# Banded attention with scores made keys by queries, shifted by maxima of rough products

## The chip, the cores and the metric

One core of a Trainium2 chip runs the whole program. The metric is the device time in microseconds (us) from start to end, the median of three runs.

## What is computed

Two layers of a hybrid block (latent attention, banded attention with a sink, a short convolution, a mixture of 16 experts), then a third block with linear and differential attention. The change touches banded attention alone. 1024 latent tokens stand beside 256 context tokens; six query heads share two key heads of 64 channels. A latent query sees all 256 context keys and the latent keys at most 128 positions away; its softmax has one more term, the head's sink. In the first layer the 256 context queries attend to the context keys too. Cut to this:

```python
valid = (jnp.abs(q_pos[:, None] - k_pos[None, :]) <= SWA_WINDOW) & ((k_pos >= 0) & (k_pos < s_len))[None, :]
s_loc = jnp.einsum('bqgrd,bkgd->bgrqk', q_b, k_b).astype(jnp.float32) * SWA_SCALE
s_loc = jnp.where(valid, s_loc, -jnp.inf)
s_ctx = jnp.einsum('bqgrd,bcgd->bgrqc', q_b, k_ctx).astype(jnp.float32) * SWA_SCALE
p = sink_softmax(jnp.concatenate([s_ctx, s_loc], axis=-1), sink).astype(v.dtype)
return (jnp.einsum('bgrqc,bcgd->bqgrd', p[..., :n_ctx], v_ctx)
        + jnp.einsum('bgrqk,bkgd->bqgrd', p[..., n_ctx:], v_b))
```

## The kernel before

The program is a row of stages, each a block in which TensorE, VectorE, ScalarE, GpSimd (POOL) and the DMA queue have their own instruction lists, tied by semaphores; a stage begins when the one before has ended on all engines. `first_half` (L1820) calls, for each of two layers, the input projection, banded attention (`window_attention`, L922), then latent attention (`latent_projections`, L1133; `latent_attention`, L1229). With `with_ctx` (first layer only) the context queries are computed as well.

Banded attention has its operands in on-chip memory: `PR` holds the projected queries and keys, channels on partitions; `SV` the values, tokens on partitions, with 64 columns of ones beside the 64 channels, so that one product gives the output and the softmax's denominator. There are no transfers in the stage. Scores must be better than one fp32r product gives, so each operand is split in a rounded part (fp32r) and the remainder. `keys` has the rounded keys twice over, on both halves of the partitions, `qs` the rounded queries in one half and their remainder in the other; their product over 128 rows (L981) is rounded keys by whole queries, and a product over 64 rows (L982) adds rounded queries by the keys' remainder (`klo`).

The work is cut in units: one head and one block of 128 queries, blocks outside, heads inside: 48 units of latent queries in each layer and 12 of context queries in the first. For a unit, TensorE (`scores`, L962) makes scores queries by keys over two context tiles and two or three band tiles (L981, L982; L984 adds a mask to the tiles at the band's ends through the identity); VectorE takes each query's maximum (`maxima`, L1088; L1092, L1093); ScalarE makes the exponentials with the maximum as bias (L1047) and the sink's (L1051); TensorE transposes them tile by tile (`turned`, L987; L993); ScalarE (L1064) and VectorE (L1119) copy the transposed tiles out; TensorE multiplies them by the values (`products`, L997; L1010) behind a product for the sink term (L1003); VectorE divides (`outputs`, L1095; L1100, L1102). An f32 product stands in the trace as two records, so that 960 stand on L1010 for 480 products. TensorE's own order is written out by hand:

```python
scores(0)
scores(1)
for u in range(N):
    turned(u)
    if u + 2 < N:
        scores(u + 2)
    products(u)
```

Scores have two double banks, transposes banks 4 and 5, outputs banks 6 and 7 in turn. Operands are rounded by ScalarE (`keys_of`, `queries`, L1027 to L1039), the remainders made by VectorE (L1078, L1085), a block ahead.

Latent attention (not changed, and the source of most durations below) is laid out otherwise: per head and half of the queries (512), rough products queries by keys with the rounded operands (`rough`, L1280; L1287) give maxima (`maximum`, L1384; L1389); they are turned into a row by products with the identity (`shift_rows`, L1290; L1295), copied by ScalarE into row 96 of the rounded queries (`shift_row`, L1345; L1348), and the exact scores, keys by queries (`exact`, L1298; L1307 to L1309), have that row subtracted by their own product; exponentials (L1361) go to the product with the values (L1317) without a transpose. `outputs` (L1398; reciprocal L1403, product L1405) take half a bank at a time.

## Time and profile before

| | |
|---|---|
| median of three runs | 4462.9 us (4458.47 to 4466.77) |
| the profiled execution | 4468.08 us, span 4466.3 us, mean granted clock of TensorE 0.941 |
| TensorE busy | 4031.1 us, 90% |
| VectorE, ScalarE, POOL busy | 2169.2 (49%), 1305.4 (29%), 517.6 us (12%) |
| banded attention, first layer | from 297.5 to 505.5 us |
| banded attention, second layer | from 1828.4 to 2011.0 us |

The page gives the busy time of each engine; a timeline gives instructions in order, TensorE's weight loads (PEld) apart from its products (PE). Products are pipelined: a product's recorded duration holds the way through the array, so what one more product costs is read from the distance of starts. A timeline merges neighbours of one line (x10). PEclk is the granted clock of TensorE, 1.00 for 2.4 GHz and 0.50 for 1.2 GHz, averaged over the stretch.

### The profile page before, as it was taken

How to read it: one execution, taken by the hardware profiler on the slowest of the kernel's cores; microseconds unless marked ns; L12 is line 12 of the kernel's file. 1: busy time of each engine (PE TensorE's matmuls, PEld its weight loads, DVE VectorE, ACT ScalarE, POOL GpSimd, SP SyncE). 2: the span in 40 equal slices, each digit the busy share in tenths (PEclk: the TensorE clock that was granted, in tenths of full speed). 3: DMA queues.
4: the chain of work that ended last, by engine and by line, in shares of the span. 5: the costliest groups of instructions: out<-in, count | busy, mean ns of one | idle time of the engine just before them, and what ended most of it. 6: DMA issues, size and time to landing. Idle time of an engine off the chain costs nothing. (4 is left out here: it accounts for less than half of the span.)

```text
span 4466.3 us, 51680 instructions
## 1 busy us (share of the span) xinstructions
PE 4031.1 (90%) x20694; PEld 3138.1 (70%) x20694; DVE 2169.2 (49%) x3350; ACT 1305.4 (29%) x2261; POOL 517.6 (12%) x600
## 2 busy tenths in 40 slices
PE   7989999887999979899987799799876999998997
PEld 5878655664777769785655799677744778887875
DVE  3567655424111156675644333475565365553444
ACT  3234533222111132344323233311354211112242
POOL 1000111102222210002111111200102100000012
PEclk8989999998999989998998899899988999999998
DMA  6000000338677541000011899312001211112111
GB/s 249 29 20 1 16 1 1 146 148 340 237 259 244 183 176 38 10 1 16 1 67 58 320 342 345 98 48 85 21 1 53 80 43 48 48 47 80 50 55 56
DMA packets 73879, 453.30 MB, mean 101 GB/s; under 512 B 8001, under 2 KB 12625, under 8 KB 57681
## 3 DMA queue, kind: packets, MB, share of 16 engines
q1 hardware_dynamic: 56960, 389.73, 23.2%
q0 software_dynamic: 13088, 47.19, 3.8%
q10 hardware_dynamic: 3632, 13.63, 0.8%
q8 instruction: 138, 2.26, 0.2%
q14 instruction: 61, 0.49, 0.0%
HBM read 394.95 MB, written 55.57 MB: 101 GB/s over the span
## 5 line engine op out<-in xcount | busy, mean ns | idle before, releaser
L2277 PEld LDWEIGHTS psum<-words,words 128*128 128x128 f32 x4096 | 515.2, 192 | 10.4 <-issue 9.1
L2277 PE MATMUL psum<-words,words 128*128 128x160 f32 (+1 forms) x4096 | 516.5, 288 | 1.4 <-DVE words L392 0.9
L675 PE MATMUL psum<-words,words 128*128 128x512 f32 x1104 | 444.1, 402 | 31.6 <-DVE words L715 27.2
L676 PE MATMUL psum<-words,words 128*128 128x512 f32 x1104 | 440.0, 399 | 0.0
L677 PE MATMUL psum<-words,words 128*128 128x512 f32 x1104 | 440.0, 399 | 0.0
L1605 PE MATMUL psum<-words,words 128*128 128x428 f32 (+1 forms) x720 | 254.0, 353 | 28.4 <-DVE words L1698 28.4
L675 PEld LDWEIGHTS psum<-words,words 128*128 128x128 f32 x1104 | 210.7, 191 | 85.4 <-DVE words L715 28.7
L1317 PE MATMUL psum<-words 128*128 128x512 f32 (+1 forms) x504 | 255.0, 588 | 0.0
L1606 PE MATMUL psum<-words,words 128*128 128x428 f32 (+1 forms) x720 | 250.7, 348 | 0.0
L1607 PE MATMUL psum<-words,words 128*128 128x428 f32 (+1 forms) x720 | 249.9, 347 | 0.0
L677 PEld LDWEIGHTS psum<-words,words 128*128 128x128 f32 x1104 | 210.5, 191 | 51.5
L676 PEld LDWEIGHTS psum<-words,words 128*128 128x128 f32 x1104 | 209.9, 190 | 51.3 <-issue 1.0
L694 ACT ACTIVATE words<-words 128x1024 fp32r<-128x1024 f32 x69 | 73.1, 1060 | 586.8 <-DMA words<-in_w_up 383.7
L1361 ACT ACTIVATE words<-psum 128x512 f32<-128x512 f32 (+1 forms) x252 | 147.8, 586 | 293.7 <-PE psum L1309 293.7
L1389 DVE TENSOR_REDUCE words<-psum 128x1 f32<-128x512 f32 (+1 forms) x300 | 163.3, 587 | 144.1 <-PE psum L1287 143.2
L792 PE MATMUL psum<-words,words 128*128 128x512 f32 (+1 forms) x448 | 174.2, 389 | 35.2 <-DVE words L515 34.8
L1307 PE MATMUL psum<-words,words 97*128 97x512 f32 (+1 forms) x252 | 191.9, 762 | 4.2 <-ACT words L1348 4.2
L591 POOL TENSOR_TENSOR words<-words 128x512 f32<-128x512 f32 (+1 forms) x56 | 76.2, 1395 | 1025.2 <-ACT words L584 1025.2
L2374 DVE TENSOR_TENSOR words<-words,psum 128x160 f32<-128x160 f32 x64 | 20.6, 321 | 319.1 <-ACT words L2337 319.1
L793 PE MATMUL psum<-words,words 128*128 128x512 f32 (+1 forms) x448 | 171.5, 383 | 0.0
L794 PE MATMUL psum<-words,words 128*128 128x512 f32 (+1 forms) x448 | 170.5, 380 | 0.0
L1605 PEld LDWEIGHTS psum<-words,words 128*128 128x128 f32 x720 | 138.4, 192 | 33.7 <-DVE words L1698 28.7
(437 smaller groups left out, 7986.1 us busy)
## 6 DMA issues: line engine op xcount, KB each, us to landing
words<-in_w_gate SPq DMA_DIRECT2D x32, 2048.0 KB
words<-in_w_up SPq DMA_DIRECT2D x32, 2048.0 KB
words<-in_w_down SPq DMA_DIRECT2D x32, 2048.0 KB, 12.7
words<-in_ada_w SPq DMA_DIRECT2D x24, 2048.0 KB, 14.6
words<-in_w_in SPq DMA_DIRECT2D x55, 512.0 KB, 3.5
words<-in_w_up SPq DMA_DIRECT2D x44, 512.0 KB, 3.4
words<-in_w_down SPq DMA_DIRECT2D x44, 256.0 KB, 2.6
words<-in_x SPq DMA_DIRECT2D x2, 5120.0 KB, 23.0
```

Source lines behind the costliest of these rows:

```text
L675: pe.matmul(out, hi[:, j, w], S.parts[0](kt, t0, nt), start=(kt == 0), stop=False)
L676: pe.matmul(out, hi[:, j, w], S.parts[1](kt, t0, nt), start=False, stop=False)
L677: mm = pe.matmul(out, lo[:, j, w], S.parts[0](kt, t0, nt), start=False, stop=(kt == KD - 1))
L792: pe.matmul(out, hi[:, j, w], x[0](kt, t0, n), start=(kt == 0), stop=False)
L793: pe.matmul(out, hi[:, j, w], x[1](kt, t0, n), start=False, stop=False)
L794: mm = pe.matmul(out, lo[:, j, w], x[0](kt, t0, n), start=False, stop=(kt == KT - 1))
L1307: pe.matmul(to, k_hi[0:ROW + 1, h % 2, key], q_hi[0:ROW + 1, h % 2, t0:t0 + n], start=True, stop=False)
L1317: pe.matmul(k.bank[O_BANK[u % 2]][:, 0:n], V[:, 6 * t + h, :], pt[:, x % R, 0:n], start=(t == 0), stop=(t == keys - 1)).then_inc(d_done, 1)
L1605: pe.matmul(out, whi[:, j, w], xhi[:, kt, c0:c0 + nc], start=(kt == 0), stop=False)
L1606: pe.matmul(out, whi[:, j, w], xlo[:, kt, c0:c0 + nc], start=False, stop=False)
L1607: mm = pe.matmul(out, wlo[:, j, w], xhi[:, kt, c0:c0 + nc], start=False, stop=(kt == KD - 1))
L2277: mm = pe.matmul(k.bank[m % 2][:, u * W:(u + 1) * W], ring[:, j, w0:w0 + P], xgT[:, j, kt, 0:W], start=(kt == 0), stop=(kt == KD - 1))
```

## The change

`window_attention` is written anew, in the manner of latent attention; nothing outside it changes. The loop now runs over heads, and in a head over steps (`body`): a step is one key tile against up to 512 queries. Context key tiles go against 512 latent queries (or the 256 context queries), a band key tile against the 384 queries that can see it (256 at the ends). 14 steps per head in the first layer, 12 in the second.

- `rough`: per query tile one product over the 256 context keys and one over the band, with rounded operands of 64 rows and the mask added; three banks (0 to 2) in a ring. VectorE's `maximum` reduces each and, when a group of queries (`parts`: 256 context queries, 512 and 512 latent ones) is complete, makes `nm`, the negative maximum (not under a floor from the sink).
- `shift_rows` turns `nm` into a row in bank 7; ScalarE's `row` copies it to row 64 of the rounded queries `q1` and makes the sink's exponential from it (`es`). `klo` has ones in row 64.
- `exact`: two products of `n` queries, rounded keys by whole queries (`keys`, `q2`, 128 rows) and remainder of the keys and ones by rounded queries and shift (`klo`, `q1`, 65 rows), and the mask for band steps; banks 3 and 4 in turn. The mask is one slice of `band_mask`, with zeros in the middle.
- `values`: the exponentials by `SV`, two steps later, into bank 5, 6 or 7, where a group's outputs stay until its last step; the group's first product spreads `es` over the denominator's rows (`to_den`, one row). Context queries of the first layer have bank 7, the shift row's, and so wait for all rows of the head (`m_row`), and `shift_rows` for the context outputs of the head before (`o_out`).
- Rough products and rows of head h + 1 stand among the steps of head h, in a hand-made order (`piece_step`, `shift_step`); those of head 0 ahead of the loop. `outputs` take 256 queries at a time and are put among the maxima by due steps.
- The transposes, their copies and the sink's product per unit are gone. Remainders are made by POOL.

The lines that are taken out are those of the kernel before, above; of the added ones the core:

```diff
+    S_BANK, C_BANK, O_BANK, M_BANK = (0, 1, 2), (3, 4), (5, 6, 7), 7
...
+    body = [st for g in range(lat + 1) for st in ctx_steps(g)]
+    body += [band_step(b) for b in range(3)] + ctx_steps(lat + 1) + [band_step(b) for b in range(3, NB)]
+    L = len(body)
+    N = H * L
...
+    piece_step = [i for i in range(L) if i not in skip][:NP]
+    shift_step = [min(max(piece_step[tiles_of[g + 1] - 1] + 2, 6), L - 1) for g in range(NG)]
...
+    for h in range(H):
+        for g in range(NG):
+            for x in range(parts[g][1] // 256):
+                outs.append((h * L + closes[g] + LAG + 0.5 + x, h, g, x))
+    outs.sort()
...
+            def rough(h, p):
+                g, t0 = query_tile[p]
+                if p == 0:
+                    pe.wait_ge(q1_set, h + 1)
+                    pe.wait_ge(k_hi, 4 if h else 1)
+                for y in range(rough_parts[p]):
+                    n = h * upto[NP] + upto[p] + y
+                    if n >= 3:
+                        pe.wait_ge(a_max, n - 2)
+                    lo, hi = (0, CT) if y == 0 else tuple(CT + b for b in band_of(t0))
+                    to = bank_of(n)[:, 0:(hi - lo) * P]
+                    mm = pe.matmul(to, q1[0:64, h % 3, t0:t0 + P], keys[0:64, h % 2, lo * P:hi * P], start=True, stop=(y == 0), skip_group_check=True)
+                    if y:
+                        pe.wait_ge(mask_set, 3)
+                        mm = pe.matmul(to, idb, masked((t0 - NCTX) // P), start=False, stop=True, skip_group_check=True)
+                    mm.then_inc(a_full, 1)
+            def shift_rows(h, g):
+                G = h * NG + g
+                pe.wait_ge(m_set, G + 1)
+                if G:
+                    pe.wait_ge(m_row, G)
+                if with_ctx and h:
+                    pe.wait_ge(o_out, o_count[h - 1, 0])
+                for x in range(parts[g][1] // P):
+                    mm = pe.matmul(k.bank[M_BANK][ROW:ROW + 1, x * P:(x + 1) * P], nm[:, h % 2, tiles_of[g] + x:tiles_of[g] + x + 1],
+                                   k.ident[:, :], start=True, stop=True)
+                mm.then_inc(m_full, 1)
+            def exact(x):
+                h, st = x // L, body[x % L]
+                t, q0, n, hide = st
+                if x % L == 0:
+                    pe.wait_ge(k_hi, 4 if h else 2)
+                    pe.wait_ge(k_lo, 2 if h else 1)
+                    pe.wait_ge(ones_set, 2 if h else 1)
+                    pe.wait_ge(q2_lo, h + 1)
+                for g in range(NG):
+                    if opens[g] == x % L:
+                        pe.wait_ge(m_row, h * NG + g + 1)
+                if x >= 2:
+                    pe.wait_ge(p_set, x - 1)
+                C, key = k.bank[C_BANK[x % 2]], slice(t * P, (t + 1) * P)
+                pe.matmul(C[:, 0:n], keys[:, h % 2, key], q2[:, h % 2, q0:q0 + n], start=True, stop=False, skip_group_check=True)
+                mm = pe.matmul(C[:, 0:n], klo[0:ROW + 1, h % 2, key], q1[0:ROW + 1, h % 3, q0:q0 + n], start=False, stop=hide is None, skip_group_check=True)
+                if hide is not None:
+                    mm = pe.matmul(C[:, 0:n], idb, hide, start=False, stop=True, skip_group_check=True)
+                mm.then_inc(c_full, 1)
+            def values(x):
+                h, st = x // L, body[x % L]
+                for g, (t0, n, bank) in enumerate(parts):
+                    if opens[g] == x % L:
+                        if h:
+                            pe.wait_ge(o_out, o_count[h - 1, g])
+                        if O_BANK[bank] == M_BANK:
+                            pe.wait_ge(m_row, (h + 1) * NG)
+                        pe.wait_ge(e_set, h * NG + g + 1)
+                        pe.matmul(k.bank[O_BANK[bank]][:, 0:n], to_den[SROW:SROW + 1, :], es[SROW:SROW + 1, h % 3, t0:t0 + n],
+                                  start=True, stop=False, skip_group_check=True)
+                pe.wait_ge(p_set, x + 1)
+                for g, c0, n, b0 in segments(st):
+                    mm = pe.matmul(k.bank[O_BANK[parts[g][2]]][:, b0:b0 + n], SV[:, 2 * st[0] + h % 2, :], pt[:, x % R, c0:c0 + n],
+                                   start=False, stop=(closes[g] == x % L), skip_group_check=True)
+                mm.then_inc(d_done, 1)
+            for p in range(NP):
+                rough(0, p)
+            pe.wait_ge(sink_set, 1)
+            for g in range(NG):
+                shift_rows(0, g)
+            pe.wait_ge(ones_set, 1)
+            for x in range(N):
+                h, i = x // L, x % L
+                exact(x)
+                if h + 1 < H:
+                    if i in piece_step:
+                        rough(h + 1, piece_step.index(i))
+                    for g in range(NG):
+                        if shift_step[g] == i:
+                            shift_rows(h + 1, g)
+                if x >= LAG:
+                    values(x - LAG)
+            for x in range(N - LAG, N):
+                values(x)
...
+            def row(h, g):
+                G, (t0, n, _) = h * NG + g, parts[g]
+                act.wait_ge(m_full, G + 1)
+                act.activation(q1[ROW:ROW + 1, h % 3, t0:t0 + n], k.bank[M_BANK][ROW:ROW + 1, 0:n], ACT.Copy).then_inc(m_row, 1)
+                act.wait_ge(m_row, G + 1)
+                act.activation(es[SROW:SROW + 1, h % 3, t0:t0 + n], q1[ROW:ROW + 1, h % 3, t0:t0 + n].bitcast(F32), ACT.Exp,
+                               bias=sink[ROW:ROW + 1, h:h + 1], scale=SWA_SCALE).then_inc(e_set, 1)
...
+            high_first(0)
+            keys_of(0, 0)
+            high_second(0)
+            keys_of(0, 1)
+            ones_of(0)
+            act.wait_ge(sink_set, 1)
+            for g in range(NG):
+                row(0, g)
+            high_first(1)
+            keys_of(1, 1)
+            keys_of(1, 0)
+            ones_of(1)
+            for x in range(N):
+                h, i = x // L, x % L
+                act.wait_ge(c_full, x + 1)
+                if x >= R:
+                    act.wait_ge(d_done, x - R + 1)
+                n = body[i][2]
+                act.activation(pt[:, x % R, 0:n], k.bank[C_BANK[x % 2]][:, 0:n], ACT.Exp, scale=SWA_SCALE).then_inc(p_set, 1)
+                if h + 1 < H:
+                    for g in range(NG):
+                        if shift_step[g] == i:
+                            row(h + 1, g)
+                    if i == 1:
+                        high_second(h + 1)
+                    if i == 3 and h + 2 < H:
+                        high_first(h + 2)
...
+            def maximum(h, p):
+                g, t0 = query_tile[p]
+                if p == 0 and h >= 2:
+                    dve.wait_ge(m_full, NG * (h - 1))
+                for y in range(rough_parts[p]):
+                    n = h * upto[NP] + upto[p] + y
+                    w = NCTX if y == 0 else (band_of(t0)[1] - band_of(t0)[0]) * P
+                    dve.wait_ge(a_full, n + 1)
+                    dve.reduce_max(pm[:, h % 2, p, y:y + 1], bank_of(n)[:, 0:w], AX.X).then_inc(a_max, 1)
+                if p + 1 == tiles_of[g + 1]:
+                    cut = slice(tiles_of[g], tiles_of[g + 1])
+                    dve.wait_ge(a_max, h * upto[NP] + upto[p + 1])
+                    m = pm[:, h % 2, cut, 0]
+                    if rough_parts[p] == 2:
+                        link(dve.tensor_tensor(mx[:, h % 2, cut], m, pm[:, h % 2, cut, 1], ALU.max))
+                        m = mx[:, h % 2, cut]
+                    dve.tensor_scalar(nm[:, h % 2, cut], m, floor[:, h:h + 1], -1.0, ALU.max, ALU.mult).then_inc(m_set, 1)
+            def outputs(n):
+                _, h, g, x = outs[n]
+                t0, _, bank = parts[g]
+                c = slice(256 * x, 256 * x + 256)
+                O = k.bank[O_BANK[bank]]
+                dve.wait_ge(d_done, h * L + closes[g] + 1)
+                if n:
+                    dve.wait_ge(o_out, n)
+                dve.reciprocal(rec[0:64, c], O[64:P, c]).then_inc(r_set, 1)
+                dve.wait_ge(r_set, n + 1)
+                dve.tensor_tensor(MIX[half(h % 2), 3 + h // 2, t0 + c.start:t0 + c.stop], O[0:64, c], rec[0:64, c], ALU.mult).then_inc(o_out, 1)
+            dve.tensor_copy(band_mask[:, 0:P], prev).then_inc(mask_set, 1)
+            dve.memset(band_mask[:, P:2 * P], 0.0).then_inc(mask_set, 1)
+            dve.tensor_copy(band_mask[:, 2 * P:3 * P], nxt).then_inc(mask_set, 1)
+            dve.tensor_scalar(sink[:, 0:H], negsink, -1.0, None, ALU.mult)
+            link(dve.tensor_scalar(floor[:, 0:H], negsink, -1.0 / SWA_SCALE, None, ALU.mult))
+            link(dve.memset(to_den[:, 0:64], 0.0))
+            dve.memset(to_den[:, 64:P], 1.0).then_inc(sink_set, 1)
+            for p in range(NP):
+                maximum(0, p)
+            due = [((h - 1) * L + piece_step[p], 0, h, p) for h in range(1, H) for p in range(NP)]
+            due += [(when, 1, n, 0) for n, (when, _, _, _) in enumerate(outs)]
+            for _, kind, a, b in sorted(due):
+                if kind == 0:
+                    maximum(a, b)
+                else:
+                    outputs(a)
```

## Rows read from the trace of the kernel before

**Rows 1.** Busy times, TensorE clock: both calls of banded attention (columns: heading line).
```profile
core 0: us, PE busy (x) PEld busy (x) DVE busy (x) ACT busy (x) POOL busy (x), PEclk, DMA share, GB/s
297.50:505.50 208.00, 194.93 (x1248) 159.20 (x1248) 153.83 (x307) 104.36 (x209) 0.00 (x0) 0.93 0.00 1
1828.40:2011.00 182.60, 172.10 (x1128) 140.42 (x1128) 129.37 (x253) 88.91 (x165) 0.00 (x0) 0.95 0.00 1
```

**Rows 2.** TensorE in order of time, one unit (start us, us, engine, line, operation).
```profile
401.02 0.36 PE L981 MATMUL psum<-words,words 128*128 128x256 f32 x1
401.31 0.38 PE L982 MATMUL psum<-words,words 64*128 64x256 f32 x1
401.62 0.38 PE L981 MATMUL psum<-words,words 128*128 128x256 f32 x1
...
402.84 0.44 PE L1003 MATMUL psum<-ident,words 128*128 128x128 f32 x2
403.12 1.28 PE L1010 MATMUL psum<-words 128*128 128x128 f32 x10
...
404.70 0.36 PE L981 MATMUL psum<-words,words 128*128 128x256 f32 x1
```

**Rows 3.** Busy times and clock (PEclk) in five short stretches, as in rows 1.
```profile
308.00:312.00 4.00, 4.00 (x15) 3.10 (x15) 1.00 (x5) 1.84 (x6) 0.00 (x0) 0.50 0.00 0
...
316.00:320.00 4.00, 4.00 (x19) 3.30 (x19) 2.90 (x7) 1.89 (x6) 0.00 (x0) 0.66 0.00 0
...
328.00:332.00 4.00, 3.66 (x22) 2.53 (x20) 3.83 (x8) 2.96 (x8) 0.00 (x0) 1.00 0.00 0
332.00:340.00 8.00, 7.64 (x29) 6.05 (x29) 4.49 (x9) 2.58 (x6) 0.00 (x0) 0.57 0.00 0
...
620.00:762.00 142.00, 137.02 (x512) 83.87 (x511) 82.02 (x140) 53.58 (x88) 17.40 (x6) 1.00 0.00 1
```

**Rows 4.** TensorE in order of time, three places of latent attention.
```profile
647.00 0.40 PE L1309 MATMUL psum<-words,words 96*128 96x512 f32 x1
647.23 1.02 PE L1317 MATMUL psum<-words 128*128 128x512 f32 x2
...
648.33 0.40 PE L1308 MATMUL psum<-words,words 96*128 96x512 f32 x1
...
650.50 0.29 PE L1308 MATMUL psum<-words,words 96*128 96x256 f32 x1
650.62 0.28 PE L1309 MATMUL psum<-words,words 96*128 96x256 f32 x1
...
2081.92 0.39 PE L1309 MATMUL psum<-words,words 96*128 96x512 f32 x1
2082.24 1.03 PE L1295 MATMUL psum<-ident,words 128*1 128x128 f32 x8
2083.20 1.12 PE L1317 MATMUL psum<-words 128*128 128x512 f32 x2
...
2101.33 1.03 PE L1295 MATMUL psum<-ident,words 128*1 128x128 f32 x8
```

**Rows 5.** Groups by line and shape, 512 to 780 us (busy us, mean ns | idle before).
```profile
L1361 ACT ACTIVATE words<-psum 128x512 f32<-128x512 f32 x100 | 59.7, 597 | 128.4 <-PE psum L1309 128.4
...
L1389 DVE TENSOR_REDUCE words<-psum 128x1 f32<-128x512 f32 x88 | 56.8, 682 | 23.1 <-PE psum L1287 22.9
...
L1403 DVE RECIPROCAL words<-psum 64x256 f32<-64x256 f32 x18 | 31.7, 1760 | 30.4 <-PE psum L1317 30.0
...
L1389 DVE TENSOR_REDUCE words<-psum 128x1 f32<-128x256 f32 x56 | 22.9, 417 | 34.4 <-PE psum L1287 34.1
...
L1405 DVE TENSOR_TENSOR words<-psum,words 64x256 f32<-64x256 f32 x18 | 7.5, 417 | 0.6
```

**Rows 6.** In order of time: ScalarE's operand copies; TensorE at the lower clock.
```profile
1829.61 5.12 ACT L1031 ACTIVATE words<-words 64x1280 fp32r<-64x1280 f32 x4
...
335.09 0.58 PE L981 MATMUL psum<-words,words 128*128 128x256 f32 x1
335.60 0.58 PE L982 MATMUL psum<-words,words 64*128 64x256 f32 x1
```

More of the change, by code:

```diff
@@ L950, in window_attention @@
-    tiles = lambda u: CT + (len(band(units[u][1])) if units[u][0] else 0)
-    second = lambda u: sum(tiles(n) > 4 for n in range(u))
-    half = lambda g: slice(64 * g, 64 * g + 64)
+    keys, klo, q1 = k.part(o, 2, NT), k.part(o + 2 * NT, 2, NT), k.part(o + 4 * NT, 3, NT)
+    es = k.at(o + 4 * NT, 3, NT)
+    o = TAB0 + 1280
+    q2, pt, rec = k.part(o, 2, NT), k.at(o + 2 * NT, R, 512), k.at(o + 2 * NT + R * 512, 512)
+    o += 2 * NT + R * 512 + 512
+    mx, nm, to_den, floor, sink = k.at(o, 2, 16), k.at(o + 32, 2, 16), k.at(o + 64, P), k.at(o + 64 + P, 8), k.at(o + 72 + P, 8)
@@ new lines, in window_attention @@
+    pm = k.at(o + 80 + P + 192, 2, 16, 2)
+    band_mask = k.at(o + 80 + P, 3 * P, dt=BF16)
+    assert o + 80 + P + 192 + 64 <= SEL0
+    half = lambda g: slice(64 * g, 64 * g + 64)
+    first = 0 if with_ctx else NCTX
+    S_BANK, C_BANK, O_BANK, M_BANK = (0, 1, 2), (3, 4), (5, 6, 7), 7
+    parts = ([(0, NCTX, 2)] if with_ctx else []) + [(NCTX, 512, 0), (NCTX + 512, 512, 1)]
+    NG = len(parts)
+    lat = NG - 2
+    tiles_of = [sum(n // P for _, n, _ in parts[:g]) for g in range(NG + 1)]
+    ctx_steps = lambda g: [(t, parts[g][0], parts[g][1], None) for t in range(CT)]
@@ L1013, in _ @@
-            scores(0)
-            scores(1)
-            for u in range(N):
-                turned(u)
-                if u + 2 < N:
-                    scores(u + 2)
-                products(u)
-        def count_t(u):
-            return u + second(u)
+            def rough(h, p):
[14 more added lines that the diff above has]
+                    mm.then_inc(a_full, 1)
@@ new lines, in _ @@
+        @block.gpsimd
+        def _(pool):
+            for h in range(H):
+                pool.wait_ge(q2_hi, h + 1)
+                pool.tensor_tensor(q2[half(1 - h % 2), h % 2, first:NT], PR[half(h % 2), SQ + h // 2, first:NT],
+                                   q2[half(h % 2), h % 2, first:NT].bitcast(F32), ALU.subtract).then_inc(q2_lo, 1)
+                if h < 2:
+                    pool.wait_ge(k_hi, 4 * h + 1 if h == 0 else 4)
+                    pool.tensor_tensor(klo[0:64, h, :], PR[half(h), SK, :], keys[half(h), h, :].bitcast(F32), ALU.subtract).then_inc(k_lo, 1)
```

201 lines of the change are left out of this document (43 added, 158 removed).

## The prediction

> **What bounds the kernel now.** I read the stretches of the two calls first, then the timeline of one unit. Banded attention runs twice, in 208.0 us for the first layer and 182.6 us for the second [rows 1], 8.7% of the span of 4466.3 us. In both TensorE is busy for 94% of the stretch and VectorE for 71 to 74%. The unit (one head, one query block) shows why: from its first score product at 401.02 to the next unit's at 404.70 are 3.68 us, and on TensorE one instruction follows the other without a gap [rows 2]. So the order of VectorE and ScalarE costs nothing in the body; what counts is what TensorE is given to do. Of the 3.68 us, 1.82 (401.02 to 402.84) are scores, 0.28 the sink term (402.84 to 403.12), 1.58 the products with the values and the next unit's transposes.
>
> The scores are dear for their size. Products of 256 columns start 0.29 to 0.31 us apart where an operand of 128 rows and one of 64 rows alternate (L981, L982) [rows 2]; in latent attention products of 256 columns that keep to 96 rows start 0.12 apart [rows 4]. I take the difference, **0.19 us, as the price of each switch** between 64 rows and the full array. An interior unit has six (into and out of L982 three times): 1.1 of its 1.82 us. From 96 rows to 128 there is no such price (L1309 at 647.00, L1317 at 647.23) [rows 4], so I give 65 rows none either.
>
> **Prices for the new work**, all at full clock. Latent attention already has the new shape (rough products, a row of maxima, scores keys by queries, products with 512 columns), so I take its spacing [rows 4]: 0.235 us for an fp32r product of 512 columns, 0.12 for 256, hence 0.18 for 384; a bf16 mask as many columns the same. An f32 product of 512 columns: 647.23 to 648.33 is 1.10, less 0.235 for L1307, so 0.86 (0.65 for 384, 0.43 for 256). The shift row of 512 queries: 2081.92 to 2083.20 is 1.28, less 0.235, so 1.05 (0.6 for 256). The sum works there: ten steps of 3 x 0.235 + 0.86, twelve rough products (8 x 0.235 + 4 x 0.12) and 1.05 give 19.1 us, and from one shift row to the next are 2101.33 - 2082.24 = 19.09.
>
> **The new body, per head, second layer.** Steps over keys: four with 512 queries, 2 x 0.235 + 0.86 = 1.33 each, 5.3 in all; six with 384, 2 x 0.18 + 0.18 for the mask + 0.65 = 1.19, 7.1; two with 256, 0.36 + 0.43, 1.6. Sum 14.0. The sink term is now one product per half with an operand of one row: 0.86 and two switches, 1.24, twice 2.5. Its price has no row; the bounds are 0.86 and 1.24, and I take the upper, as one row is further from 128 than 64 is. Rough products: 256 columns, then 384, then the mask, with the 64-row operand entered and left once: 0.12 + 0.18 + 0.18 + 0.38 = 0.86 for six query tiles, 0.74 for the two at the ends, 6.6 in all. Shift rows 2 x 1.05 = 2.1. So 16.5 for exact scores and values and 8.7 for rough products and shift rows; the latter of head 0 lie ahead of the loop: 6 x 16.5 + 5 x 8.7 = **142.7 us**. In the first layer the context queries add 1.34 (two steps of 256 queries), 0.8 (sink), 1.0 (two rough tiles) and 0.6 (shift row): 6 x 18.7 + 5 x 10.3 = **163.9 us**. What is removed is the whole old body: the transposes, their eviction by ScalarE (L1064) and VectorE (L1119), 48 or 60 sink products, and four of six switches.
>
> **The other engines** lie beside that. VectorE, second layer, per head: a maximum over 256 columns 0.42, over 512 0.68, so some 0.55 over 384; ten of the first and six of the second are 7.5. Four outputs of 1.76 + 0.42 are 8.7 (one reciprocal of 64x256 takes 1.76), small ones 1.2: 17.4 against 25.2 on TensorE [rows 5]. ScalarE: exponentials 4 x 0.60 and less for the others, 6; two operand copies 2.1; copy and exponential of the row 2.4: under 11. POOL's two remainders were VectorE's and take 2 to 3 us each, a head ahead. None bounds the sum, but VectorE's outputs come in pairs of 4.4 us, and **the ring of three banks** lets TensorE run only three maxima ahead. By the hand-made order of the second layer the pair of the first half is ready at the end of step 10; VectorE is at the next head's first maximum 4.7 us later and has it at 5.1, while TensorE wants that bank (second part of the second tile) at 4.7: a wait of 0.6. In the first layer the pair of the last half is ready 4.6 us after the end of step 12, ends at 9.9, and the maximum of the third tile is done at 10.4 where TensorE wants its bank at 8.6: a wait of 1.9. Behind the waiting product stand the values of two steps earlier and all exact scores, so it is lost. Over four head changes: **3 and 8 us**. The new waits on the shift row's bank (the context output must have left it, all rows of the head must have been copied) come five steps or more after what they wait for: nothing.
>
> **The opening** is new and longer. Now TensorE starts when the first half of the operands is there, and every engine alternates from then on. After: two ScalarE copies at 1.28 us (5.12 for four) [rows 6], then all rough products of head 0 at half clock, since TensorE has been idle, and its clock is at 0.50 (1.2 GHz) at this place today [rows 3]. Cold, a switched product of 256 columns takes 0.51 [rows 6] (0.21 of columns, so 0.3 a switch); a tile is 0.51 + 0.33 + 0.62 = 1.5, the ends 1.3: 11.5 us, or 12.3 with the context. Then the shift rows, one after the other: 2.0 us cold (8 x 0.21 + 0.3), the row's copy 0.6, 0.2 of signals: 5.4, or 7.2. Then ScalarE has the row's exponential and three operand copies (0.6 + 1.1 + 2.5) before the rough product of head 1 may run, which stands ahead of the second step on TensorE. Sums: 2.6 + 11.5 + 5.4 + 4.2 = 23.7, and 2.8 + 12.3 + 7.2 + 4.4 = 26.7; less the step done meanwhile, **23.5 and 26.5 us**. The clock: today it comes back 11 us or so after dense work starts (0.50 from 308 to 312, 0.66 from 316 to 320, full from then on [rows 3]); I give the loop the same 11 us at half speed, 5.5 lost in each layer (bounds 0 and 8). **The end** is two outputs behind the last product, 0.3 + 2 x 2.2 = 4.7.
>
> **Sum.** Second layer 142.7 + 3 + 23.5 + 5.5 + 4.7 = 179.4 against 182.6. First layer 163.9 + 8 + 26.5 + 5.5 + 4.7 = 208.6 against 208.0. Together -2.6 us. The profiled execution took 4468.1 us (span 4466.3), 5.2 over the median of 4462.9; so 4465.5 for such an execution and **4460 us** for the median. What the transposes and most switches gave, the rough scores, the shift rows and a serial opening take.
>
> **Rivals.** (1) **Switches cost nothing in the new order.** The 0.19 is read from products of 256 and fewer columns that alternate each time. If it vanished for products entered once per tile, the loop would lose 0.38 per tile and sink product: 5 x 3.8 + 6 x 1.1 = 25.8 and 5 x 3.0 + 6 x 0.8 = 19.8, the openings 10, while some 8 come back as waits for the ring: -48 us, 4412; at half that price 4436. For it: the alternation in the row is closer than in the new code. Against: both directions of the switch show it in [rows 2], and it is the same at 0.5 of the clock [rows 6]. The Trainium skill, "TensorE: Matmul & The Clock Gate", section "Step-by-step: what each phase is for", says that the weights of the next product are loaded while the current one runs, and that the number of rows does not matter for the load; by that rule alone this rival is the forecast. The trace agrees where rows stay at 96 or more [rows 4] and disagrees at 64 [rows 2], so the measurement decides.
> (2) **The clock falls inside the loop** (slower). TensorE was busy for 3.66 of 4 us from 328 to 332, waiting a little in each unit, and the next 8 us ran at 0.57 of the clock, which costs 3.4 us [rows 3]. If each of the eight head changes with its wait did the same, that is 8 x 3.4 = 27 us: 4488. From four such falls on the change is slower by more than a measurement's doubt. Against: latent attention, of the same shape, ran at 1.00 through 142 us (620 to 762), in which TensorE was idle for 5 [rows 3].
> (3) **More waits in the ring and between the engines** than by hand: 1 us more per head in both layers, 12 us: 4472.
> (4) The opening overlaps better (clock back during the rough products): 10 us less, 4450.
>
> **Chances.** Forecast (4451 to 4469) 0.32; (1) 0.28, mostly between 4412 and 4445; (4) 0.08; (2) 0.18; (3) 0.14. A measurement of this kernel can tell some 0.2%, 9 us, from no change: faster 0.36, same 0.32, slower 0.32. The range of 8 in 10 leaves out the far half of (1) and what lies beyond (2): 4425 to 4488; the likeliest case alone has 4451 to 4469.
>
> **What would show it.** Right: a body step of 512 queries without rough work at 1.33 us; a rough tile at 0.86 between its neighbours; the sink product at 1.24; no first exact product before 19 us into the stage. Wrong: a rough tile near 0.5, a sink product of 0.9 (rival 1); PEclk under 0.9 past the first 15 us of the loop (rival 2); TensorE waiting for the maxima for more than 2 us per head, or for exponentials at all (rival 3). The exact scores' second product has 65 rows: if it too pays a switch, each step costs 0.38 more and both layers together 59 us; the 96-row rows speak against it.

## The result, and the profile after

The changed kernel takes 4475.4 us (median of 12 runs, 4467.2 to 4482.0) where the kernel before, in 12 runs, takes 4466.8: a ratio of 1.0022 [1.0015, 1.0029], slower by 8.5 us. The forecast was 4460 us, some 3 us faster than the kernel before. The profiled execution has a span of 4469.8 us. Windows of the kernel after, columns as in rows 1: both stages; then each opening (to the first rough product of head 1), the start of the loop, and its rest:

```profile
297.80:516.70 218.90, 193.54 (x720) 107.28 (x720) 121.97 (x205) 85.27 (x139) 23.09 (x8) 0.85 0.00 1
1842.20:2021.10 178.90, 163.08 (x624) 91.29 (x624) 100.99 (x175) 73.52 (x115) 19.80 (x8) 0.88 0.00 1
...
297.80:324.70 26.90, 16.32 (x48) 8.02 (x49) 11.72 (x30) 14.74 (x16) 5.77 (x2) 0.50 0.00 0
324.70:345.00 20.30, 20.28 (x67) 11.28 (x68) 8.82 (x19) 9.53 (x15) 5.73 (x2) 0.80 0.00 1
345.00:509.50 164.50, 156.94 (x608) 87.97 (x605) 94.75 (x151) 61.01 (x109) 11.59 (x4) 0.92 0.00 1
1842.20:1864.50 22.30, 14.96 (x43) 7.20 (x43) 9.10 (x27) 13.25 (x14) 5.24 (x2) 0.50 0.00 1
1864.50:1890.00 25.50, 25.50 (x69) 13.17 (x69) 6.92 (x16) 9.29 (x14) 5.19 (x2) 0.65 0.00 0
1890.00:2013.60 123.60, 122.25 (x516) 70.92 (x514) 77.94 (x126) 50.97 (x88) 9.37 (x4) 1.00 0.00 1
```

The first two answer to [rows 1]: the first layer has gone from 208.0 to 218.9 us, the second from 182.6 to 178.9. So the second is as forecast (179.4) and the first 10 us off. The others say where. A stretch of length t at PEclk c had 2 x (1 - c) x t at the lower clock, and half of that is lost. In the first layer that is 8 us at the start of the loop and, past 345, where the kernel before had a clock of 1.00, 27.3 us more (from windows of 4 us; 0.92 is rounded). Past 345 TensorE is also idle for 164.50 - 156.94 = 7.5 us. In the second layer the low clock lasts 18 us into the loop, and after 1890 the clock is at 1.00 to the end.

| us | first layer, forecast | measured | second, forecast | measured |
|---|---|---|---|---|
| opening | 26.5 | 26.9 | 23.5 | 22.3 |
| TensorE's work in the loop | 163.9 | 159.5 | 142.7 | 139.2 |
| lost to low clock at its start | 5.5 | 4.0 | 5.5 | 8.9 |
| waits for the ring | 8 | 7.5 | 3 | 1.4 |
| **lost to low clock later** | **0** | **13.7** | **0** | **0** |
| end | 4.7 | 7.1 | 4.7 | 7.1 |
| stage | 208.6 | 218.8 | 179.4 | 178.9 |

(Work in the loop is what is left of it after the other rows.) What the waits are and where the clock falls, the kernel after shows at every head change of the first layer. In order of time (start us, us, engine, line, operation; in brackets the idle time before and its releaser), and the windows around it:

```profile
392.12 1.76 DVE L1182 RECIPROCAL words<-psum 64x256 f32<-64x256 f32 x1
...
394.76 0.38 PE L1011 MATMUL psum<-words,words 64*128 64x256 f32 x1
...
396.23 0.42 DVE L1184 TENSOR_TENSOR words<-psum,words 64x256 f32<-64x256 f32 x1
396.68 0.76 DVE L1164 TENSOR_REDUCE words<-psum 128x1 f32<-128x256 f32 x2
...
397.16 0.43 PE L1011 MATMUL psum<-words,words 64*128 64x384 f32 x1 [2.01 <-DVE words L1164]
```
```profile
392.00:396.00 4.00, 3.15 (x15) 1.95 (x13) 3.83 (x4) 2.73 (x4) 2.89 (x1) 1.00 0.01 2
396.00:400.00 4.00, 2.84 (x5) 0.83 (x5) 3.87 (x8) 0.00 (x0) 0.00 (x0) 0.69 0.01 4
400.00:404.00 4.00, 4.00 (x9) 2.15 (x8) 0.47 (x2) 0.49 (x1) 0.00 (x0) 0.50 0.00 0
404.00:408.00 4.00, 4.00 (x18) 1.99 (x18) 1.13 (x3) 1.83 (x4) 0.00 (x0) 0.96 0.00 0
```

VectorE does the pair of outputs (two reciprocals, each with its product, 392.12 to 396.65) before the maximum that would free the bank; the rough product waits 2.01 us for it. Then the granted clock is at its lower level for 2 x (0.31 + 0.50 + 0.04) x 4 = 6.8 us, and 3.4 us go. Of the four such places two have a wait of 2.01 us and two one of 1.76: 7.5 + 4 x 3.4 = 21.1 us.

### The profile page after: what moved, and what is told of

Its sections match the earlier page's. It is cut to its first block and busy times, and to the rows that moved or that the text cites. A ratio compares the mean times of both kernels' runs of the same rounds, so it can differ in the third digit from the quotient of the medians.

```text
span 4469.8 us, 49160 instructions
## 1 busy us (share of the span) xinstructions
PE 4017.5 (90%) x19662; PEld 3036.6 (68%) x19662; DVE 2110.7 (47%) x3170; ACT 1271.9 (28%) x2141; POOL 558.1 (12%) x616
## 5 line engine op out<-in xcount | busy, mean ns | idle before, releaser
L794 PE MATMUL psum<-words,words 128*128 128x512 f32 (+1 forms) x448 | 171.2, 382 | 0.0
```

The costliest lines, as they stand in the source:

```text
L794: mm = pe.matmul(out, lo[:, j, w], x[0](kt, t0, n), start=False, stop=(kt == KT - 1))
```

## The experiments

The theory: the four waits of the first layer turn into clock falls, and without them the change would be faster than the kernel before; in the second layer the waits are too short for it. Rivals: the falls are bound to something else at these places (the loop's rhythm, power) and the waits cost only their own 7.5 us; or the switch price is wrong and the loop is slow for that. Ratios are to the kernel before on the same chip.

**e1_outputs_spread**: the last half's second output and the context output are done later in VectorE's order, in the first layer alone.
```
-                outs.append((h * L + closes[g] + LAG + 0.5 + x, h, g, x))
+                late = 0 if not with_ctx else (2.2 if (g, x) == (2, 1) else 1.1 if g == 0 else 0)
+                outs.append((h * L + closes[g] + LAG + 0.5 + x + late, h, g, x))
```


> First layer only: on VectorE the last half's second output of a head moves behind the maxima of the third and fourth query tile, the context output behind those of the fourth. Theory A (the wait for the ring of maxima at the head change makes TensorE idle 2 us, and its clock then falls to 1.2 GHz for some 7 us): idle gaps and falls at the four head changes of the first layer vanish, 4 x (2.0 + 3.4) = 22 us less than the changed kernel, stage of the first layer from 219 to some 198 us. Theory B (the clock falls because the head change has narrow work: 256-query steps, products with one and 64 rows): the falls remain, only the wait goes, 8 us less. Theory C (the order shifts the wait to the shift row or to the context output): within 3 us. The second layer stays at 179 us in all three.

Measured: 4457.1 us (11 runs), 0.9979 [0.9970, 0.9988]: faster than the kernel before. The first stage takes 201.4 us, the second 178.9, as in the kernel after. Its loop past 345:
```profile
345.00:490.80 145.80, 145.80 (x621) 84.65 (x619) 96.21 (x155) 62.17 (x111) 11.59 (x4) 1.00 0.00 1
```
No idle time of TensorE and no fall after 345. The stage gained 17.4 us and not 21.1, because the clock came back 9 us later in the opening (43.8 us at the lower level in the first 48 us of the stage, where the kernel after has 34.9), which costs 4.5. Waits and falls vanish together; that they are cause and effect needs e9.

**e9_fill_wait**: the order of VectorE stays; TensorE fills the wait with seven products of 512 columns that nobody reads, into a bank that is free at that time.
```
+                    if with_ctx and h >= 2 and (p, y) == (3, 1):
+                        x = (h - 1) * L + 4
+                        pe.wait_ge(p_set, x)
+                        for _ in range(7):
+                            pe.matmul(k.bank[C_BANK[(x + 1) % 2]], keys[:, 0, 0:P], q2[:, (h - 1) % 2, NCTX:NCTX + 512], start=True, stop=True, skip_group_check=True)
```


> First layer: at four head changes TensorE runs seven products without use (512 columns, 1.6 us, into the free score bank) exactly where it waits 2 us for the ring of maxima now. The wait as time stays, only the idleness goes. Theory A (it is the idleness that makes the clock fall): TensorE's idle time there goes under 0.5 us, PEclk stays at 1.00, 4 x 3.4 = 14 us less than the changed kernel. Theory B (the narrow work around it makes the clock fall): falls stay, no change within 3 us.

Measured: 4467.2 us (11 runs), 1.0001 [0.9992, 1.0010]. First the loop past 344, then one head change (the second L1011 line is this kernel's filler, L1016 its rough product):
```profile
344.00:501.00 157.00, 156.60 (x658) 91.50 (x658) 97.39 (x158) 63.64 (x114) 11.62 (x4) 1.00 0.00 1
```
```profile
396.53 0.38 PE L1016 MATMUL psum<-words,words 64*128 64x256 f32 x1
396.84 1.88 PE L1011 MATMUL psum<-words,words 128*128 128x512 f32 x7
398.92 0.44 PE L1016 MATMUL psum<-words,words 64*128 64x384 f32 x1 [0.20 <-DVE words L1169]
```
The next head's work comes no sooner than before, 2.4 us after the rough product ahead of it, and the clock stays at 1.00 throughout. So at these four places TensorE's idleness is the cause of the falls, and the maxima only of the idleness. The first stage took 210.1 us: 8.7 less, of the 13.7 lost to the falls, because here too the opening was 9.1 us longer at the lower clock (-4.6); why is not shown.

In the second layer, which is the same code, two falls came (3.4 and 6.8 us at the lower level; 183.5 us for the stage), each some 3 us behind a wait of 0.38 us. The second of them:
```profile
1964.88 0.44 PE L1016 MATMUL psum<-words,words 64*128 64x384 f32 x1 [0.38 <-DVE words L1169]
```
```profile
1967.60:1971.60 4.00, 4.00 (x9) 2.00 (x10) 3.39 (x5) 0.49 (x1) 0.72 (x1) 0.50 0.01 2
```
The kernel after, e1, e3 and e5 have the same two waits of 0.38 us there and no fall behind them. So a short wait is no guarantee of a full clock, and the theory's word on the second layer does not hold as it stands; what decides is not shown.

**e2_stall_second**: two fills of 128x1280 on VectorE behind the last half's second output, in heads 0 to 3 of the second layer.
```
+                if not with_ctx and (g, x) == (1, 1) and h < 4:
+                    for _ in range(2):
+                        link(dve.memset(k.at(XT0 + 7 * NT, NT), 0.0))
```


> Second layer only: VectorE gets two memsets of 1.3 us each (unused memory) after the last half's second output of heads 0 to 3, so that TensorE waits for the ring as long there as in the first layer. Theory A (a wait of 2 us is followed by a fall of the clock): PEclk drops to 0.5 for some 7 us at the four head changes of the second layer, which has none now; 4 x (2.1 + 3.4) = 22 us more than the changed kernel. Theory B (falls come from the narrow work of the first layer's head change, which the second lacks): only the wait, 8 us more, clock at 1.00. If VectorE has more slack than worked out: less than 5 us more.

Measured: 4488.7 us (4 runs), 1.0052 [1.0037, 1.0068]; the second stage takes 195.1 us, 16.2 more. One of the four waits (2.58 or 2.70 us each), then the windows around them, first those of the first and third wait, then those of the second and fourth:
```profile
1936.43 0.44 PE L1011 MATMUL psum<-words,words 64*128 64x384 f32 x1 [2.70 <-DVE words L1164]
```
```profile
1906.00:1912.00 6.00, 3.74 (x17) 2.35 (x18) 4.25 (x10) 1.20 (x2) 0.00 (x0) 1.00 0.00 0
1964.00:1972.00 8.00, 6.07 (x28) 3.73 (x28) 4.28 (x9) 2.74 (x5) 0.00 (x0) 1.00 0.00 0
1936.00:1946.00 10.00, 9.57 (x32) 5.27 (x33) 4.08 (x10) 2.99 (x5) 0.00 (x0) 0.83 0.00 0
1996.00:2006.00 10.00, 10.00 (x29) 4.61 (x27) 1.96 (x4) 2.85 (x5) 0.00 (x0) 0.69 0.00 0
```
Idle time in the loop rose by 10.6 us. The clock fell behind the second and fourth wait, not behind the first and third. A wait of this size brings a fall there in two cases of four; it makes one possible, not certain. In the first layer, by contrast, each of the four waits had a fall behind it in this run too.

**e3_operands_early**: ScalarE makes the operands of head 1 before it copies the shift row of head 0.
```
-            act.wait_ge(sink_set, 1)
-            for g in range(NG):
-                row(0, g)
             high_first(1)
...
             ones_of(1)
+            act.wait_ge(sink_set, 1)
+            for g in range(NG):
+                row(0, g)
```


> Both layers: ScalarE makes the operands of head 1 (four copies, 4.9 us) before the shift rows of head 0, where it is idle for 10 us now, rather than behind them. Theory A (TensorE's idle stretch of 4.6 us before the first rough product of head 1 is these copies): 4.5 us less per layer, and the clock returns earlier after the opening, another 2 to 5 us in all: 9 to 14 us less than the changed kernel. Theory B (the loop waits for something else at its beginning, such as the remainders made by POOL or the row's exponential): under 4 us less.

Measured: 4462.4 us (11 runs), 0.9994 [0.9985, 1.0003]; stages 213.9 and 175.1 us, 4.9 and 3.8 less. The kernel after, then e3, at the first rough product of head 1:
```profile
324.72 0.55 PE L1011 MATMUL psum<-words,words 64*128 64x256 f32 x1 [4.62 <-issue]
```
```profile
320.26 0.58 PE L1011 MATMUL psum<-words,words 64*128 64x256 f32 x1
```
The 4.62 us are gone ("issue" in the row names no releaser; that ScalarE's copies are it, the experiment shows). The four falls at the head changes stayed, 27.3 us: they have nothing to do with the opening.

**e4_rough_65**: the rough products read 65 rows, the 65th of the queries being zero, so that the maxima are the same. For head 0 both copies of the keys must then be there, so ScalarE makes the second one before `high_second(0)`.
```
-                    mm = pe.matmul(to, q1[0:64, h % 3, t0:t0 + P], keys[0:64, h % 2, lo * P:hi * P], ...
+                    mm = pe.matmul(to, q1[0:ROW + 1, h % 3, t0:t0 + P], keys[0:ROW + 1, h % 2, lo * P:hi * P], ...
...
+                act.activation(q1[ROW:ROW + 1, h % 3, first:NT].rearrange("p (a n) -> p a n", n=P), wide[:, 0:(NT - first) // P, :], ACT.Copy, scale=0.0)
```


> The rough products read 65 rows of the queries and keys in place of 64; the added row of the queries is zero, so the result is the same. ScalarE has one more copy of 1.1 to 1.3 us per head and the first rough product comes 2.5 us later in each layer. Theory A (entering and leaving an operand of 64 rows costs a switch, 0.28 us per query tile by the trace after): tiles of 0.47 in place of 0.75, 11 to 13 us less in each layer's loop and 4 in each opening, minus the 2.5, minus some 3 us of longer waits for the ring in each: 18 to 24 us less in all. Theory B (the spacing has another cause, such as the fp32r weights behind a bf16 mask): no tile changes, 5 us more from the later start.

Measured: 4470.3 us (11 runs), 1.0009 [0.9999, 1.0019]. A rough tile of the kernel after, then of e4, each from the score ahead of it to the values behind it:
```profile
375.18 0.39 PE L1044 MATMUL psum<-words,words 65*128 65x512 f32 x1
375.50 0.56 PE L1011 MATMUL psum<-words,words 64*128 64x256 f32 x2
...
376.16 0.81 PE L1062 MATMUL psum<-words 128*128 128x384 f32 x2
```
```profile
1932.80 0.34 PE L1046 MATMUL psum<-words,bmask 128*128 128x384 bf16 x1
1932.84 0.59 PE L1011 MATMUL psum<-words,words 65*128 65x256 f32 x2
...
1933.45 0.59 PE L1062 MATMUL psum<-words 128*128 128x256 f32 x2
```
With 64 rows the tile takes 376.16 - (375.18 + 0.235) = 0.75 us, with 65 rows 1933.45 - (1932.80 + 0.18) = 0.47. The switch price is real, 0.28 for a tile, and one more row removes it. But the time hardly moved: the first stage is even longer, 224.0 us from its first instruction, the added copy (the profiled execution was 6.6 us over this kernel's median), the second shorter, 175.3. Over the loop of the first layer TensorE waits 22.8 us for the ring in four waits of up to 5.8, where the kernel after has 7.5, and the time at the lower clock past the opening rose from 27.3 to 41.0 us. Part of it is that TensorE comes to the ring earlier. The larger part is VectorE, at each of the four head changes; here at the first:
```profile
358.12 2.90 POOL L1147 TENSOR_TENSOR words<-words,words 64x1280 fp32r<-64x1280 f32 x1 [22.09 <-ACT words L1098]
358.18 2.86 DVE L1173 TENSOR_SCALAR words<-words 128x2 f32<-128x2 f32 x1
...
365.98 0.69 PE L1011 MATMUL psum<-words,words 65*128 65x384 f32 x1 [5.64 <-DVE words L1165]
```
The small operation that makes the context queries' shift takes 2.86, 2.75, 2.87 and 2.73 us there, and in the loop of the kernel after 0.23. It starts just behind a subtraction of POOL and ends with it; from its end VectorE works without a gap (two outputs, then the maximum) until TensorE's wait is over. That is 10.3 of the 15.3 us of added waits, by VectorE's rows; no run moved POOL's instruction in this kernel. In the second layer the waits grew to 0.73 and 0.86 us, and two of them had a fall behind them (10.2 us at the lower level in all; the kernel after: none). So a gain on TensorE was given back twice, as a wait and as a fall.

**e5_sink_97**: the sink product reads 97 rows, 96 of them zero, instead of one; `es` gets a buffer of its own, one deep instead of three, and POOL clears it once.
```
-                        pe.matmul(k.bank[O_BANK[bank]][:, 0:n], to_den[SROW:SROW + 1, :], es[SROW:SROW + 1, h % 3, t0:t0 + n],
+                        pe.matmul(k.bank[O_BANK[bank]][:, 0:n], to_den[0:SROW + 1, :], es[0:SROW + 1, t0:t0 + n],
...
+            pool.memset(es[0:SROW, :], 0.0).then_inc(zeroed, 1)
```


> The sink product reads 97 rows (96 of them zero) in place of the one row 96; everything else as in the changed kernel, the result is the same. In the trace after it takes 1.05 us from its start to the first product with the values, against 0.86 for an f32 product of 512 columns. Theory A (a switch on one side is paid, 0.19 us): 6 x (3 + 2) x 0.19, 5 to 6 us less in all. Theory A' (both sides are paid as I took in the forecast, the second seen only in the product behind it): 11 us less. Theory B (the 1.05 is the length of the f32 product behind a mask): no change. In all of them the falls of the clock in the first layer stay.

Measured: 4455.2 us (7 runs), 0.9972 [0.9961, 0.9983]; stages 213.8 and 171.1 us. The kernel after, then e5, from sink product to values, behind a mask:
```profile
494.05 0.28 PE L1046 MATMUL psum<-words,bmask 128*128 128x256 bf16 x1
494.27 1.12 PE L1058 MATMUL psum<-words,words 1*128 1x512 f32 x2
495.32 1.12 PE L1062 MATMUL psum<-words 128*128 128x512 f32 x2
```
```profile
489.99 0.28 PE L1047 MATMUL psum<-words,bmask 128*128 128x256 bf16 x1
490.11 1.02 PE L1059 MATMUL psum<-words,words 97*128 97x512 f32 x2
490.97 1.02 PE L1063 MATMUL psum<-words 128*128 128x512 f32 x2
```
One row costs 495.32 - (494.05 + 0.12) = 1.15 us, 97 rows 490.97 - (489.99 + 0.12) = 0.86: 0.29 for a product, between theories A and A'. Much of the second stage's 7.8 us is not this: the clock came back 10 us sooner there (29.7 us at the lower level in place of 40.1), which is 5.2.

**e6_context_later**: in a head, five band steps instead of three come before the last context steps, so that the first half closes sooner.
```
-    body += [band_step(b) for b in range(3)] + ctx_steps(lat + 1) + [band_step(b) for b in range(3, NB)]
+    body += [band_step(b) for b in range(5)] + ctx_steps(lat + 1) + [band_step(b) for b in range(5, NB)]
```


> Both layers: the two context steps of the last half stand behind the fifth band step rather than behind the third, so the first half's outputs are ready two steps (2.5 us) earlier in each head. Theory A (VectorE's outputs, waiting in a row, set both the wait for the ring at head changes and the end of the stage): the end of each layer, 7.5 us from the last product to the last output, gets 2.3 to 2.5 shorter, twice; at each head change of the first layer the wait of 2.0 us goes to under 0.5 and with it most falls of the clock: 4 x (1.7 + 3.4) = 20 us; together 20 to 25 us less than the changed kernel. Theory B (the last half's two outputs and the context output alone make the wait): only the ends gain, 5 us less.

Measured: 4458.5 us (11 runs), 0.9980 [0.9971, 0.9989]; stages 212.7 and 174.0 us. The end is 4.9 us in both, after 7.5 when it is read in the same way (from the start of the last product). In the kernel after, four outputs queue there, not two: one every 2.3 us. The first and the last of VectorE's rows at the end of the first layer:
```profile
507.44 1.76 DVE L1182 RECIPROCAL words<-psum 64x256 f32<-64x256 f32 x1 [8.30 <-PE psum L1062]
...
516.17 0.42 DVE L1184 TENSOR_TENSOR words<-psum,words 64x256 f32<-64x256 f32 x1
```
The waits sank to 4.7 us in all, of 1.1 and 1.2 us each and not under 0.5 as expected, and behind each of the four the clock still fell (17 us at the lower level in all).

**e8_five** joins e1, e3, e4, e5 and e6; **e10_four** is the same without e4 (rough products of 64 rows).

> The five edits together: outputs spread among the maxima, operands of head 1 early, rough products of 65 rows, sink product of 97 rows, context steps later. If they add up by their own measured gains (18 in the first layer's order, 9 from early operands, 10 to 20 from the rough products once no clock falls eat it, 5 from the sink, 5 from the end) the time is 40 to 50 us under the changed kernel's, 4425 to 4435, and some 35 under the kernel before: no fall of the clock inside the loops. If VectorE becomes the bound (21 us per head in the first layer plus its waits, against 25 on TensorE): 25 to 35 us under the changed kernel, with TensorE waiting for maxima 1 us or more per head and falls of the clock coming back.

> The kernel with the five edits, but its rough products read 64 rows again (no zero row, first rough product as early as in the changed kernel). Run to price the 64-row operand where no fall of the clock and no long wait blurs it. Theory A (0.28 us per query tile, two switches): in the first layer 5 x (8 x 0.28 + 2 x 0.2) = 13 us more, in the second 11, and in the openings some 2 less to 2 more: 20 to 26 us more than the five edits. Theory B (the spacing has another cause): within 5 us of the five edits.

Measured: e8 4400.6 us (5 runs), 0.9850 [0.9837, 0.9864]; e10 4421.6 us (5 runs), 0.9904 [0.9889, 0.9919]. The loops of both layers, e8 and then e10:
```profile
327.90:462.90 135.00, 134.90 (x649) 89.96 (x647) 101.58 (x165) 69.34 (x121) 12.68 (x5) 1.00 0.00 1
...
1823.10:1941.20 118.10, 115.67 (x545) 75.64 (x544) 81.69 (x134) 56.53 (x96) 9.43 (x4) 1.00 0.00 1
```
```profile
328.90:481.50 152.60, 152.60 (x653) 92.45 (x653) 104.34 (x166) 65.01 (x117) 12.75 (x5) 0.98 0.00 1
1839.10:1966.10 127.00, 126.56 (x547) 75.07 (x547) 83.51 (x135) 54.27 (x94) 9.39 (x4) 1.00 0.00 1
```
With the waits gone from the first layer's loop (2.4 us of them are left in the second, none over 0.7, and no fall) the 65th row is worth its price: TensorE's busy time in the second layer is 126.56 - 115.67 = 10.9 us less, 0.27 for each of 40 tiles; in the first layer 17.7, of which 3 are e10's lower clock, so 0.29 for each of 50. Alone (e4) it brought 5 us, on top of the others 21 by the medians and 24 by the ratios. The stages of e8 take 171.2 and 154.1 us, 36.8 and 28.5 less than before the change: it is the fastest version, 66 us under the kernel before and 75 under the kernel after. That is 24 us better than the best that was expected of it: the five edits' own changes of the two stages add up to some 48 us, those of e8 to 72. Alone, e4 had lost to waits and falls what it gave, and e1 and e6 had openings 9 us longer at the lower clock in the first layer, where e8 has 28.6 us at it and the kernel after 34.9.

**e11_port**: e8, with POOL's first remainder held back until VectorE's first shift is made. In the first layer's opening of the kernel after, one small operation of VectorE took 2.62 us beside POOL's (2.82 in e8):
```profile
301.50 2.88 POOL L1146 TENSOR_TENSOR words<-words,words 64x1280 fp32r<-64x1280 f32 x1 [5.37 <-ACT words L1097]
...
301.78 2.62 DVE L1172 TENSOR_SCALAR words<-words 128x2 f32<-128x2 f32 x1
```
```
+                if with_ctx and h == 0:
+                    pool.wait_ge(m_set, 1)
```


> The five edits, and in the first layer POOL starts the remainders of head 0 only when VectorE has made the first shift (a tensor_scalar of 128x2 elements in on-chip memory, which lasted 2.82 us while POOL's 2.88 us subtraction of 64x1280 ran, against 0.23 at any other time). Theory A (the two engines share a port, and VectorE's instruction waited for POOL's): the tensor_scalar takes 0.23, TensorE's 2.5 us of waiting there vanish, the opening of the first layer is 2 to 2.5 us shorter, the time at most 2.5 us less. Theory B (it is long for another reason, such as the first use of that instruction in the stage): it stays at 2.8 us and nothing changes.

Measured: 4400.3 us (5 runs), 0.9852 [0.9838, 0.9865], no gain over e8 (timed apart from it; stages 170.8 and 153.8). VectorE and POOL of e11:
```profile
302.86 0.23 DVE L1182 TENSOR_SCALAR words<-words 128x2 f32<-128x2 f32 x1
...
306.21 2.88 POOL L1160 TENSOR_TENSOR words<-words,words 64x1280 fp32r<-64x1280 f32 x1
...
307.14 1.96 DVE L1180 TENSOR_TENSOR words<-words 128x4 f32<-128x4 f32 x1
```
The first operation now takes 0.23, but the next, 0.16 elsewhere, takes 1.96 and ends with POOL's second. The wait has only moved.

Not tried: outputs that read a bank of which TensorE still writes the other half, which would spread them without a change of the order.

## Why the prediction was wrong

**The step that failed** is the clock inside the loop, taken at nothing: the loss to it past the start measured 13.7 us in the first layer. The wait itself was worked out right (1.9 us; measured 1.76 and 2.01 in turn), and rival (2) had its price right (3.4 us for each). The prediction let the rival go with "latent attention ran at 1.00 through 142 us, in which TensorE was idle for 5". That was a sum over a stretch. Its longest single gaps are two of 1.03 us, and the wait that I had worked out myself was nearly twice that in one piece. One of the two, in the kernel before:
```profile
659.42 1.10 PE L1287 MATMUL psum<-words,words 96*128 96x512 f32 x2 [1.03 <-DVE words L1389]
```
 The row that spoke for the rival, a fall right after small gaps [rows 3], was the nearer one; the gaps there are of 0.30 to 0.56 us, one in each unit. In this kernel it held in the first layer alone: 13.7 us for four head changes. In the second the waits came out at 0.4 us at most (forecast 0.6) and no fall followed. Had the four falls been priced, the first layer's sum would have been 222.2 and the total 4473.6; that this lies so near to 4475.4 is in part luck, since the work was 4.4 and 3.5 us less than forecast and the ends and the second loop's low clock together 8 more. The sign that was written down for the rival, PEclk under 0.9 past the first 15 us of the loop, would have missed the falls: it is 0.92 there.

**Right**: the openings (26.9 and 22.3 for 26.5 and 23.5), the 65-row second score without a switch, and the step's price. In the kernel after,
```profile
499.44 0.69 PE L1043 MATMUL psum<-words,words 128*128 128x512 f32 x1
...
500.56 0.63 PE L1043 MATMUL psum<-words,words 128*128 128x384 f32 x1
```
a step of 512 queries with values of 384 takes 1.12 = 2 x 0.235 + 0.65, as the prices had it. **Rival (1) is false**: switches cost 0.28 a tile, entered once, in two different orders (e4; e10 against e8), where the forecast had 0.38 and the rival nothing. The Trainium skill, "TensorE: Matmul & The Clock Gate", section "Step-by-step: what each phase is for", has the row count not matter for the weight load. For the load itself the kernel after agrees: from 375 to 390 a load takes 184 ns on average with 64 rows, 182 with one, 190 with 65 and with 128. What 64 rows or one cost stands in the distance to the next product's start, which the prediction had set against that rule; a load of the same length does not make the switch free.

**Mis-sized terms.** The rough tile: 0.75 for 0.86, as the way in behind a mask or score costs less than 0.19 (375.50 less 375.415 is 0.09). The sink product: 1.15 for 1.24, the upper bound. Over 50 or 40 tiles and the sink products both come to some 7 and 5 us, and the work of the loops was lower by 4.4 and 3.5, so that 2 us or so were added that I have not followed. The end: 7.1 for 4.7, because the steps of the last head go without rough products and are short, so that the first half's outputs are not out of the way; e6 moved it to 4.9. The low clock at the second loop's start: 8.9 lost for 5.5. Two slips that move nothing: by its own terms the first layer's work is 6 x 18.7 + 5 x 10.3 = 163.7 us, not 163.9; and a switch is not the same at half clock but 0.3 us for 0.19 [rows 6].

**The sum.** The stages went up by 10.9 and down by 3.7, 7.2 in all, and the medians by 8.5; the spans of the two profiled executions differ by 3.5, so the rest of the program was 3.7 faster in this one execution. The experiments' medians likewise moved by up to 8 us more than their stages (e3: 13 for 8.7). A difference of 5 us is read from the stages, not from the medians.

**Open**: why the clock comes back in the opening after 24 to 44 us at the lower level in kernels whose TensorE work there is nearly the same (after 34.9, e1 and e9 44, first layer), why two of e2's four waits left it alone, and why it fell behind two waits of 0.38 us in e9 and of 0.73 and 0.86 in e4 and behind no other wait under 1 us in the second layers.

## What to carry to other kernels

Where a sum contains a wait of TensorE of more than 1 us in one piece, price a clock fall with it (mostly 3.4 us here) as likely: in the first layers of six kernels (the kernel after and e2 to e6) each of 24 waits of 1.1 to 5.8 us had one behind it, in e2's second layer two of four. Look at the longest gap in a row that speaks against it, not at the sum of gaps. Shorter waits are not safe either: of 41 of 0.17 to 0.86 us in the second layers four had a fall behind them. In an order written by hand, put VectorE's long outputs behind the maxima that free a bank; faster products before that is done come back as waits (e4: 5 us alone, 21 once the waits were gone). After each edit look again at which small operations now lie beside a long one of another engine: e4's waits grew most by that. Where 64-row operands alternate with full ones, try a 65th row of zeros.

## What the runs showed of the hardware

Two things I had not expected. A 65th row makes a rough tile (two products and a mask) cheaper: 0.47 us instead of 0.75. And an operation of VectorE on 128x2 elements in on-chip memory took 2.62 us beside a subtraction of POOL, 0.23 without one, and ended with it, while a reciprocal from an accumulation bank kept its 1.76 beside the same subtraction (392.12, with POOL's from 392.07 for 2.89). The Trainium skill, "SBUF — State Buffer", section "Who interferes with whom", tells of a port that the two share and that one of them holds for its whole instruction; the rows agree, and e11 shows that moving POOL's instruction moves the wait to the next such operation. What it costs in the opening is not shown, as the wait only moved; in e4's loop it stood ahead of the maximum that TensorE waited for.
